# Output projection of a hybrid decoder block: four half-products over 1024 replaced by seven products of quarter blocks

## The reference, cut to what matters

```python
h = rms_norm(x, norm_ffn1_g);  x = x + 0.5 * swiglu_ffn(h, w_ffn1_up, w_ffn1_down)
h = rms_norm(x, norm_mix_g);   u, v, gates = split(h @ w_in)
y_a = glu(gelu(s5_ssm(u)) @ w_ssm_glu)
y_b = silu(layer_norm(depthwise_conv(v))) @ w_conv_pw
x = x + (sigmoid(g_a) * y_a + sigmoid(g_b) * y_b) @ w_out      # the output projection
h = rms_norm(x, norm_ffn2_g);  x = x + 0.5 * swiglu_ffn(h, w_ffn2_up, w_ffn2_down)
return rms_norm(x, norm_final_g)
```

## Time and profile before

| | us |
|---|---|
| median of 3 runs | 2189.06 (2188.43 to 2189.15) |
| the profiled execution, its own time | 2189.07 |
| its span | 2187.3 |
| PE busy / DVE / ACT / POOL | 2148.9 / 1670.9 / 942.4 / 630.9 |
| OUTP stage, first to last of its matmuls | 1443.9 to 1538.0 of the span |

### The profile page before, as it was taken

One profiled execution on the slowest core, in us unless ns is written; L12 is line 12 of the kernel. 1 busy time (PEld: TensorE's weight loads), 2 busy tenths in 40 slices (PEclk: granted clock), 3 DMA queues, 4 the chain that ended last, 5 costly groups with the idle time before them and its releaser, 6 DMA issues.

```text
span 2187.3 us, 31579 instructions
## 1 busy us (share of the span) xinstructions
PE 2148.9 (98%) x10239; PEld 1775.7 (81%) x10239; DVE 1670.9 (76%) x2123; ACT 942.4 (43%) x1552; POOL 630.9 (29%) x717
## 2 busy tenths in 40 slices
PE   7999999999999999999999999999999999999998
PEld 6788888888878888888887788887878888888886
DVE  5877877879995999999998559364587777665557
ACT  5455555544455222222224225044355555544444
POOL 2887645969980000000000420000024442000000
PEclk9999999999999999999999999999999999999999
DMA  5235876488774344544445622563256664337764
GB/s 172 77 120 180 269 225 201 154 292 295 251 266 146 104 142 133 161 145 144 150 141 163 202 82 93 181 211 107 73 174 211 223 213 157 105 117 261 232 195 173
DMA packets 307650, 379.60 MB, mean 174 GB/s; under 512 B 27762, under 2 KB 200402, under 8 KB 307441
## 3 DMA queue, kind: packets, MB, share of 16 engines
q1 hardware_dynamic: 287024, 306.27, 43.8%
q0 software_dynamic: 18800, 67.85, 9.3%
q10 hardware_dynamic: 1744, 4.46, 0.5%
HBM read 258.42 MB, written 120.08 MB: 173 GB/s over the span
## 4 chain that ended last, share of the span: by engine, by line
PE 87%; DVE 7%; ACT 2%; DMA 2%; issue 1%; SPq 0%; ACTq 0%; DVEq 0%
PE PU L1412 11%; PE PU L1413 11%; PE PU L1414 11%; PE PU L1352 9%; PE PU L1354 9%; PE PU L1353 9%; PE PD L1286 3%; PE PD L1287 3%; PE PD L1288 3%; PE PU L1286 3%; PE PU L1287 3%; PE PU L1288 3%; PE PD L1488 1%; PE PD L1490 1%; PE PD L1489 1%
## 5 line engine op out<-in xcount | busy, mean ns | idle before, releaser
L1352 PE MATMUL PU<-Hhi,Whi 128*128 128x512 f32 x896 | 352.3, 393 | 2.0 <-issue 1.7
L1354 PE MATMUL PU<-Hhi,Wlo 128*128 128x512 f32 x896 | 348.8, 389 | 0.0
L1353 PE MATMUL PU<-Hlo,Whi 128*128 128x512 f32 x896 | 348.7, 389 | 0.0
L2508 DVE SCALAR_TENSOR_TENSOR XT<-XT,wq 128x1024 f32<-128x1024 f32 x240 | 312.9, 1304 | 8.2
L1352 PEld LDWEIGHTS PU<-Hhi,Whi 128*128 128x128 f32 x896 | 168.2, 188 | 40.1 <-issue 4.5
L1354 PEld LDWEIGHTS PU<-Hhi,Wlo 128*128 128x128 f32 x896 | 168.2, 188 | 35.2
L1353 PEld LDWEIGHTS PU<-Hlo,Whi 128*128 128x128 f32 x896 | 168.3, 188 | 34.9 <-issue 0.7
L1412 PE MATMUL PU<-Hhi,Dhi 128*128 128x512 f32 x480 | 187.0, 389 | 0.4 <-ACT s1b L1765 0.4
L1413 PE MATMUL PU<-Hlo,Dhi 128*128 128x512 f32 x480 | 186.7, 389 | 0.0
L1414 PE MATMUL PU<-Hhi,Dlo 128*128 128x512 f32 x480 | 186.7, 389 | 0.0
L1286 PE MATMUL PD<-Dhi,Ahi 128*128 128x512 f32 x352 | 137.6, 391 | 2.1 <-DVE Alo L2094 1.7
(11 more groups left out here) (405 smaller groups left out, 5192.1 us busy)
## 6 DMA issues: line engine op xcount, KB each, us to landing
TAB<-in_w_ffn_down POOLq DMA_DIRECT2D x44, 512.0 KB, 4.9
d_sb<-TAB POOLq DMA_DIRECT2D x44, 512.0 KB, 3.7
Wraw<-in_w_ffn_up SPq DMA_DIRECT2D x80, 256.0 KB, 3.8
XT<-in_w_ffn_up SPq DMA_DIRECT2D x80, 256.0 KB, 5.1
d_sa<-XT SPq DMA_DIRECT2D x80, 256.0 KB, 2.4
Wraw<-in_w_in SPq DMA_DIRECT2D x32, 512.0 KB, 5.2
d_act<-G SPq DMA_DIRECT2D x48, 256.0 KB, 2.5
WRd<-d_sb SPq DMA_DIRECT2D x44, 256.0 KB, 4.4
```

Source lines behind the costliest of these rows:

```text
L1352: mm(o_, Whi[s][:, side, k, :], Hhi[:, k, hs[h]], start=k == 0, stop=False)
L1353: mm(o_, Whi[s][:, side, k, :], Hlo[:, k, hs[h]], start=False, stop=False)
L1354: last = mm(o_, Wlo[s][:, side, k, :], Hhi[:, k, hs[h]], start=False, stop=k == KT - 1)
L2508: stt(CVb, z_, w_, CVb, ALU.mult, ALU.add).then_inc(m["conv"], 1)
```

## The change

OUTP becomes seven products in Winograd's form, like the down projections, with 4 steps instead of 11: 7 x 4 x 12 = 336 matmuls of 128x512. In detail:

- Products in the order x = 2, 1, 5, 6, 3, 7, 4. The first two split their left operand straight from the merged tiles in XT; those of the other five (a merged quarter `d_m` and four sums `d_ms`) are stored to HBM by SP and loaded again. DVE forms the sums in `merged_sums(n)` after each PW round: in the Alo buffer for rounds 0 to 2, in TAB for the last.
- POOL forms the four weight combinations of each pair of w_out rows in the buffers of Ahi and Dhi, after the last split before PW (`p_lo`), and stores them (`d_wo`).
- The splits of Hhi/Hlo from the merged tiles go (16 hi on ACT, 16 lo on DVE). The first four steps of OUTP are split by ACT and DVE within PW's last round; ACT first waits for the stores of rounds 0 to 2 and for all weight stores.
- The residual rows come in four quadrants of 1 MB instead of two transfers of 2 MB; `gather` adds each product to its quadrants.
- Scaled rows of the first half go to an idle buffer (`Hrow`, the second half of Hhi), not back into XT. Their first transposes stand in the seventh product, the second ones in FFN2's first plain product.

```diff
-OUTP = Proj(KT, 7 * FI, None, 7, 7 * (FI - 1))
+OT = KT // 2
+OUTP = Proj(OT, 7 * FI, 7, 7 * (FI - 1))
+XN_IN_H = (("nf2", 0),)
+    WOr = over("Ahi", 0, "WOr0", [P, 2, D]), over("Dhi", 0, "WOr1", [P, 2, D])
+    Hrow = over("Hhi", 0, "Hrow", [P, KT, L])
+    MSr = over("Alo", 0, "MSr", [P, 4, HW])
+    msum = lambda n, x: MSr[:, x, :] if n < OT - 1 else at4(TAB, 2 + x)
+    M_STORES = 16 * 5
+    merged = lambda p, t: XT[:, 2 * t + (1 if D_ORD[p] == 2 else 0), 0:HW]
...
 # SP, in round n of PW
             pw_io(n)
+            if n:
+                store_merged_sums(n - 1)
+                store_merged(n - 1)
...
 # SP, after PW's rounds
-        def residuals():
-            sp.wait_ge(b_["m_lo"], 2 * KT)
-            for h in range(2):
-                load_rows(OUTP, h, d_x)
+        sp.wait_ge(m_st, M_STORES * (OT - 1))
+        load_rows(0, 1)
+        for t in range(OT - 1):
+            load_merged(2, t)
+        for t in range(OT):
+            load_out_weights(1, t)
+        sp.wait_ge(b_["m"], 4 * OT)
+        store_merged_sums(OT - 1)
+        store_merged(OT - 1)
+        sp.wait_ge(ra_lo, OUTP.z0 + OT + 2)
+        sp.wait_ge(mx_ld[0], 32)
+        load_rows(0, 0)
+        for p in range(2, 7):
+            for t in range(OT):
+                if (p, t) == (2, OT - 1):
+                    sp.wait_ge(m_st, M_STORES * OT)
+                if p > 2 or t == OT - 1:
+                    load_merged(p, t)
+                load_out_weights(p, t)
+                if (p, t) == (2, OT - 1):
+                    sp.wait_ge(ra_lo, OUTP.z0 + 2 * OT)
+                    load_rows(1, 0)
+                if (p, t) == (3, 1):
+                    sp.wait_ge(mx_ld[1], 32)
+                    load_rows(1, 1)
...
 # POOL
+        wo_load(0)
+        wo_load(1)
+        pool.wait_ge(b_["p_lo"], 2 * KT)
+        for t in range(OT):
+            (b12, b11), (b22, b21) = [halves(WOr[t % 2][:, i, :]) for i in range(2)]
+            wo_loaded(t, 0)
+            step(g.tensor_tensor(b11, b12, b11, ALU.subtract))
+            wo_loaded(t, 1)
+            step(g.tensor_tensor(b12, b22, b12, ALU.subtract))
+            step(g.tensor_tensor(b22, b22, b11, ALU.subtract))
+            step(g.tensor_tensor(b21, b22, b21, ALU.subtract))
+            for i in range(2):
+                pool.dma_start(d_wo[t, 2 * i:2 * i + 2].rearrange("a p n -> p a n"), rows_p(WOr[t % 2][:, i, :])).then_inc(wo_st[t % 2][i], 16)
+            if t + 2 < OT:
+                wo_load(t + 2)
...
 # PE
+        def out_proj():
+            for p in range(6):
+                for t in range(OT):
+                    proj_step(OUTP, p, t)
+            for js in ((0, 1), (2, 3)):
+                for t in range(OT):
+                    proj_step(OUTP, 6, t, js, js[-1] == 3)
+                    if (js[0], t) == (2, 1):
+                        turn("nf2", 0, 0)
...
-                pe.wait_ge(x_add, X0[FFN2] - 2)
-            plain_half(S, r0, 0, 0, ready)
+                pe.wait_ge(*norm_at("nf2", "lo", 2))
+                plain_half(S, r0, 0, 0, ready, {1: lambda: turn(name, 0, 1)})
+                pe.wait_ge(*norm_at("nf2", "lo", 4))
...
 # ACT, slot_free of OUTP's first steps
                 act.wait_ge(m["u_full1"], KT)
+                act.wait_ge(m_st, M_STORES * (OT - 1))
+                for n in (OT - 2, OT - 1):
+                    for i in range(2):
+                        act.wait_ge(*wo_stored(n, i))
...
+        def out_proj():
+            for p in range(1, 6):
+                for t in range(OT):
+                    split_step(OUTP, p, t)
                 if p == 2:
+                    quadrant(OUTP, 0, 1, 1, 0)
+            quadrant(OUTP, 0, 0, 4, 4)
+            split_step(OUTP, 6, 0)
+            split_step(OUTP, 6, 1)
+            act.wait_ge(*norm_at("nf2", "rs", RS_STEPS["nf2"]))
+            scaled_rows("nf2", OUTP, 0, (0, 1))
+            split_step(OUTP, 6, 2)
+            scaled_rows("nf2", OUTP, 0, (2, 3))
+            act.wait_ge(x_st, 16 * (J + 4))
+            split_step(OUTP, 6, 3)
+            quadrant(OUTP, 1, 0, 5, 8)
+            turned("nf2", 0, 0)
+            quadrant(OUTP, 1, 1, 6, 12)
+            turned("nf2", 0, 1)
...
 # DVE
+        def out_proj():
+            for p in range(1, 6):
+                for t in range(OT):
+                    split_step(OUTP, p, t)
+                if p in (1, 3, 4):
+                    dve.wait_ge(mx_ld[p == 3], 48 if p == 4 else 32)
+                for j in range(4):
+                    gather(OUTP, p - 1, j)
+                if p == 2:
+                    split_pair(R_FFN2 + 1, (KT // 2 - 1) % 2)
+            split_step(OUTP, 6, 0)
+            row_scale("nf2", 0)
+            for t in range(1, OT):
+                split_step(OUTP, 6, t)
+            dve.wait_ge(mx_ld[1], 48)
+            for j in range(4):
+                gather(OUTP, 5, j)
+            gather(OUTP, 6, 0)
+            gather(OUTP, 6, 1)
+            turned("nf2", 0, 0)
+            gather(OUTP, 6, 2)
+            gather(OUTP, 6, 3)
+            turned("nf2", 0, 1)
...
 # DVE, PW's rounds
             for h in range(2):
+                if n == KT // 2 - 1 and h == 1:
+                    for t in range(RING):
+                        split_step(OUTP, 0, t)
...
-                if n == KT // 2 - 1:
-                    lo_half(h, b_["m_hi"], b_["m_lo"])
-            split_pair(R_PW + n + 2, n % 2)
+            merged_sums(n)
+            if n < KT // 2 - 1:
+                split_pair(R_PW + n + 2, n % 2)
```

More of the change, by code:

```diff
@@ L78 @@
 ADDS = 4 * sum(len(to) for to in D_TO.values())
-X0 = {FFN1: 0, OUTP: ADDS, FFN2: ADDS + 16}
-D_ADDS = {S: [X0[S] + 4 * sum(len(D_TO[x]) for x in D_ORD[:p]) for p in range(8)] for S in (FFN1, FFN2)}
+X0 = {FFN1: 0, OUTP: ADDS, FFN2: 2 * ADDS}
+D_ADDS = {S: [X0[S] + 4 * sum(len(D_TO[x]) for x in D_ORD[:p]) for p in range(8)] for S in (FFN1, OUTP, FFN2)}
 KEPT = (FI + 1, 2 * FI)
@@ L331, in build @@
     T_AT = {1: (RB[1], 5), 2: (RB[2], 6), 3: (RB[3], 7), 4: (RB[4], 4)}
-    junk = G[0][:, :]
+    junk = {FFN1: G[0][:, :], OUTP: at4(tf, 2), FFN2: G[0][:, :]}
     def xo(S, h, j):
@@ L438, in alone @@
         eng.sem_inc(passed, 1)
[L441 to L449, removed]
     @block.sync
@@ L1630, in quadrant @@
                 n = 4 * h + j
-                fn(junk, xo(S, h, j)[:, hs[dh]], ACT.Square, accum_out=tok[:, 4 * dh, n:n + 1]).then_inc(sq, 1)
-                if S is FFN1 and (h, dh) == (0, 0):
-                    act.dma_start(d_x[j], xo(S, 0, j)).then_inc(x_st, 16)
+                fn(junk[S], xo(S, h, j)[:, hs[dh]], ACT.Square, accum_out=tok[:, 4 * dh, n:n + 1]).then_inc(sq, 1)
+                if S is not FFN2 and (h, dh) == (0, 0):
+                    act.dma_start((d_x if S is FFN1 else d_x2)[j], xo(S, 0, j)).then_inc(x_st, 16)
         def down(S, behind):
@@ L1722, in plain_silu @@
             wait(act, act_saved[h], r * 16 + saved0[h])
+            if S is FFN2 and r == 0:
+                act.wait_ge(ra_lo, FFN2.z0)
             fn(G[h][:, :], PU[r][0][:, :], ACT.Silu).then_inc(g_ready[h], 1)
@@ L2088, in split_step @@
             n, turn_, slot = step_at(S, p, t)
+            at = place(S, slot)
             dve.wait_ge(rd_hi, n + 1)
-            at = place(S, slot)
             tt(at4(dlf, at), raw_d(S, at), f32(at4(df, at)), ALU.subtract).then_inc(rd_lo, 1)
-            if S.a0 is not None:
-                dve.wait_ge(ra_hi, n + (S.a0 - S.z0 + 1))
-                tt(at4(alf, at), raw_a(S, at), f32(at4(af, at)), ALU.subtract).then_inc(ra_lo, 1)
+            dve.wait_ge(ra_hi, n + 1)
+            src = merged(p, t) if S is OUTP and p < 2 else raw_a(S, at)
+            tt(at4(alf, at), src, f32(at4(af, at)), ALU.subtract).then_inc(ra_lo, 1)
         def rsqrt(dst, src, eps, chain, room=(NV, NT), between={}):
```

243 lines of the change are left out of this document (120 added, 123 removed).

## The result

The changed kernel took 2177.66 us (median of 5 runs, 2176.12 to 2179.32), the kernel before 2189.12 (5 runs, 2188.43 to 2190.32): a ratio of 0.9947, 95% interval [0.9937, 0.9958]. Forecast were 2178.0 and a range from 2174.0 to 2185.0. The profiled execution took 2176.12, span 2174.0.

What follows compares the result with a forecast made beforehand. The output projection stage was taken as bound by PE. Matmuls 10.9 plus old gaps 3.5 less new gaps 3.3 made 11.1 us off 2189.07, so 2178.0, with a range from 2174.0 to 2185.0.

Steps and rivals of the forecast that it cites:

- What goes: 10.9 + 3.5: In the output projection, 48 fewer matmuls save 10.9 us of PE and two vanished idle gaps save 3.5 us.
- Both old gaps: PE idle in the old stage: 1.1 us behind a queued w_out load, 2.4 us behind rows awaiting a d_x store.
- The gate: 1437.5: Before OUTP's first split, ACT waits for stores of round 2's merged sums until 1437.5; 4.4 us later would still cost nothing.
- DVE's four additions a round: 2.6 us: In each PW round, DVE's extra additions take about 2.6 us, hidden in its 8.1 us wait for PE.
- POOL done by 1412, or 1423 beside DVE: POOL's weight sums ahead of the stage land by 1412, or 1423 if DVE stretches its 16 additions, before the 1437.5 gate.
- The middle at zero: Products 0 to 5 stall PE for zero: DVE needs at most 9.5 us per product of 10.9.
- The seventh product: 0.7, 1.8, 0.8: In product 6, PE idles 0.7 us at step 2, 1.8 at step 3 and 0.8 at the transposes, 3.3 together.
- Spare time of the second half's rows: 2.1 us: Second-half rows are scaled by T+40.1, PE wants them at T+42.2 in FFN2's second plain product: 2.1 us to spare.
- No new gaps: Rival: ACT's and DVE's jobs at the end overlap better, so 14.4 us off, 2174.7; chance 0.12.
- Late gate or loads: Rival: gate past its slack or middle waiting for loads; 4 us lost gives 2182.0, 8 us 2186.0; chance 0.20.
- Slower by POOL: Rival: POOL's additions wait for DVE's pair splits, PE starts the stage at 1467, time 2201; chance 0.05.
- Caught in FFN2: Rival: saved PE time is caught by DVE in FFN2's start, up to half lost, 2183.5; chance 0.03.

Runs made afterwards that it cites:

- the two edits of the kernel before: Kernel before with the second 2 MB of residual rows loaded a phase later: 2187.74 us; kernel before with first-half row stores issued behind their scaling: 2186.51 us.
- The two experiments in which such stalls came: Changed kernel with scaled rows in place instead of in the idle buffer: 2178.77 us; changed kernel with POOL's weight sums two rounds later: 2194.36 us.

## Why the prediction was right

- **What bounds the kernel.** PE, as said. Taking 48 matmuls more out of the middle took 8.6 us off.
- **What goes: 10.9 + 3.5.** The spacing is 0.2270 us against 0.2268. Both old gaps came from the waits named, as the two edits of the kernel before show.
- **The gate: 1437.5, 6.4 us ahead of a stage put at 1443.9.** Measured 1435.40, 6.25 ahead of a stage that started at 1441.65, ended by the store `d_m<-XT`, the merged stores and not POOL's, as forecast. The agreement is partly luck: the last of the merged stores was priced from one rate.
- **DVE's four additions a round: 2.6 us.** True of round 2, without POOL (1422.88 to 1425.50). In rounds 0 and 1, beside POOL's additions, they took 5.9 and 6.4. It cost nothing, as DVE had 8.1 us of waiting for PE in a round; the forecast had looked for this contention on POOL's side alone.
- **POOL done by 1412, or 1423 beside DVE.** It issued its last stores from 1413.39, and stores issued there took 8.7 us to land, so near 1423. Two errors met. POOL's 16 additions were stretched by some 4.8 us in all (25.6 against 16 of 1.3), less than the bound of 11, and the reload after the second pair's stores waited 6.38 us, where I had 3.6. The timeline of POOL, and the landing by kind in the view of the DMA queues from 1385 to 1420 (KB each, median us to landing):

```profile
1394.54 0.57 POOL L1282 DMA_DIRECT2D WOr<-in_w_out  x1 [6.38 <-DMA d_wo<-WOr]
...
1409.87 3.23 POOL L1299 TENSOR_TENSOR WOr<-WOr 128x512 f32<-128x512 f32 x1
1413.39 1.46 POOL L1301 DMA_DIRECT2D d_wo<-WOr  x2 [0.30 <-POOL WOr L1299]
```

```profile
DMA packets 7321, 11.94 MB, mean 341 GB/s; under 512 B 444, under 2 KB 4249, under 8 KB 7318
d_wo<-WOr POOLq DMA_DIRECT2D x6, 512.0 KB, 8.6
```

  A landing of 8.6 us at 341 GB/s against 3.6 in a quiet stretch: the price was taken from the wrong surroundings, and it cost nothing only because the gate hung on another store.
- **The middle at zero.** Right: no gap in 299 spacings. The loads came closer to it than the forecast had: ACT waited 2.61 us for a load of weight sums at 1456.55, inside the 8 us that a split has.
- **The seventh product: 0.7, 1.8, 0.8.** Measured 1.29, 1.66, 0.57, 3.5 against 3.3. The mechanism is the one named, and taking it away by the order of splits and rows gave 3.0 and 3.5 us back. The first was undersized: its scaled rows started a little later than the series had them.
- **Spare time of the second half's rows: 2.1 us.** They were scaled by 1532.69 + 4.27 = 1537.0, and PE's transposes of them start at 1538.84: 1.9.
- **Sum: 11.1.** 11.2 and 11.4 from the stage on in two profiles; 11.5 by the medians (2189.12 less 2177.66). With the measured gaps the terms give 10.9 + 3.5 - 3.5 = 10.9; the rest, 0.3 to 0.5, lies in a stretch of FFN2 that no term named (24.85 us from 1581.25 on, against 25.33 from 1594.03 on before). So that the last tenths agree is luck.
- **The rivals.** No new gaps: false here, and the runs with the splits first are that case, 2174.6 and 2175.2 against its 2174.7. Late gate or loads: no gap of PE from either. Slower by POOL: real as a mechanism, but it needs POOL to start two rounds later. Caught in FFN2: false, since nothing of the gain was lost behind the stage.

Where the account has a hole: the profiled execution was 1.9 us under the forecast, about what it gained ahead of the stage. The stage started between 1443.25 and 1444.19 in three kernels that have the old PW, and between 1441.19 and 1444.40 in those with the new one. The two overlap, so whether the edit gives anything there, or only falls into this spread, stays open.

The worst of the prices was not in the sum: what a longer stall of PE costs. I put the old store wait and a late gate at the length of the stall. The two experiments in which such stalls came cost 2.3 and 2.6 us more.

## What to carry to other kernels

When an engine bound by matmuls loses some, count the saving at the spacing of starts, then write the serial work of the other engines at the seam as a list with times; where two jobs of one engine meet there, put first what PE wants first. Price a transfer from a stretch whose DMA load is the one it will meet, and give each gate its slack, since it is the slack that decides what an error in its time is worth. Before taking out a wait, look at what else ends at nearly the same time: the profile names only the last.

## What the runs showed of the hardware

- **A stall can cost more than its length.** After gaps of 0.24 and 2.08 us with six matmuls between them the granted clock fell to 0.50 (1.2 GHz), and ten spacings behind the next gap were 0.426 us: 2.3 us more. After a standstill of 14.9 us the price was 2.6. With gaps of 1.29 and 1.66 us, and in the kernel before with the single gap of 2.4, it stayed at 1.00. Why the one pair of gaps was enough is not shown.
- **DVE and POOL hold each other up.** DVE's 2.29 us subtraction took 3.38 us from 1408.56 on, and POOL's addition, 1.3 us while DVE idled (at 1366.98), 3.23 from 1409.87 on. The Trainium skill (SBUF — State Buffer, Who interferes with whom) says that a DVE instruction with two SBUF inputs and a GpSimd one that reads SBUF exclude each other, the second waiting for the whole of the first. The trace agrees: POOL's addition before this one ended at 1409.79, and 1409.79 + 2.29 = 1412.08 is nearly DVE's end at 1411.94, behind which POOL's needs its 1.3 (1413.24; it ended at 1413.10). One addition of DVE, 2.60 us instead of 0.69 from 1404.34 on, partly beside an issue of POOL's stores, is not explained by this.
